# A transformer pair on one core: state products taken apart, gates issued earlier, heads scored in pairs

## The reference, cut to what matters

```
S_t = S_(t-1) diag(decay_t) + (S_(t-1) (-kk_t)) (kk_t a_t)^T + v_t k_t^T
y_t = S_t r_t
merged = sigmoid(gate_sb) * (y_sb @ w_sb_out) + sigmoid(gate_rw) * (y_rw @ w_rw_out)
h = h + merged @ w_out;   h = h + ffn(rms_norm(h));   h = rms_norm(h)
```

## Time and profile before

| what | value |
|---|---|
| three runs | 2570.83, 2576.66, 2577.05 us; median 2576.66 us |
| the profiled execution, its own time | 2576.99 us |
| its span in the profile | 2574.1 us |
| mean granted clock of TensorE | 0.981 |
| PE busy over the span | 97% |
| HBM read, written | 400.40 MB, 17.83 MB |

### The profile page before, as it was taken

How to read it: one execution, slowest core, us unless ns; L and a number is a source line. 1 busy time by engine, 2 the same in 40 slices (tenths; PEclk the granted TensorE clock), 3 DMA queues, 4 the chain that set the end, 5 groups by cost and what they waited for, 6 DMA issues and landing times.

```text
span 2574.1 us, 43775 instructions
## 1 busy us (share of the span) xinstructions
PE 2488.6 (97%) x17359; PEld 2250.1 (87%) x17359; DVE 1725.5 (67%) x3063; ACT 1248.0 (48%) x2655; POOL 534.9 (21%) x423
## 2 busy tenths in 40 slices
PE   7898999999999999999999999999999999999997
PEld 6768897999779999999888887779999999888886
DVE  4647324445668876888777555668876888777556
ACT  5441133544545454444555554555454444555554
POOL 3600142454437800000000000437700000000000
PEclk9999899999999999999999999999999999999999
DMA  5400024666325666565688666324665655777664
GB/s 172 139 9 1 18 98 155 180 185 189 119 69 152 184 184 183 182 181 182 211 244 245 196 193 190 115 82 148 186 183 183 183 181 182 213 244 240 196 192 153
DMA packets 148074, 421.07 MB, mean 164 GB/s; under 512 B 15904, under 2 KB 49056, under 8 KB 147488
## 3 DMA queue, kind: packets, MB, share of 16 engines
q1 hardware_dynamic: 144080, 405.34, 51.7%
q0 software_dynamic: 2192, 8.99, 1.0%
q10 hardware_dynamic: 1600, 3.96, 0.4%
HBM read 400.40 MB, written 17.83 MB: 162 GB/s over the span
## 4 chain that ended last, share of the span: by engine, by line
PE 86%; DVE 8%; DMA 3%; ACT 3%; issue 1%; DVEq 0%; ACTq 0%
PE pb L424 85%; DMA raw<-in_vT 2%; PE pb L433 1%; DVE arena L1475 1%; ACT arena L1054 1%; DVE arena L1478 1%; ACT hi L1042 1%; DVE lo L1485 1%; DVE arena L1625 1%; ACT L1054 0%; DMA H<-in_x 0%; DVE WL L2200 0%; DVE arena L2173 0%; DVE sm L1475 0%; DVE arena L1557 0%
## 5 line engine op out<-in xcount | busy, mean ns | idle before, releaser
L1042 ACT CAST hi<-raw 128x512 fp32r<-128x512 f32 x1402 | 816.8, 620 | 397.0 <-PE pb L424 180.8
L424 PE MATMUL pb<-HTh,hi 128*128 128x256 f32 (+1 forms) x2968 | 859.0, 289 | 0.2
L424 PE MATMUL pb<-HTl,hi 128*128 128x256 f32 (+1 forms) x2968 | 843.7, 284 | 0.0
L424 PE MATMUL pb<-HTh,lo 128*128 128x256 f32 (+1 forms) x2968 | 843.1, 284 | 0.0
L2236 POOL TENSOR_TENSOR lo<-raw,hi 128x512 fp32r<-128x512 f32 x383 | 514.0, 1364 | 646.2 <-ACT hi L1042 645.9
L1485 DVE TENSOR_TENSOR lo<-raw,hi 128x1024 fp32r<-128x1024 f32 x464 | 565.0, 1218 | 83.9 <-ACT hi L1042 83.9
L424 PEld LDWEIGHTS pb<-HTh,hi 128*128 128x128 f32 x2968 | 571.5, 193 | 2.4 <-DVE arena L1475 0.7
L424 PEld LDWEIGHTS pb<-HTl,hi 128*128 128x128 f32 x2968 | 572.1, 193 | 1.0
L424 PEld LDWEIGHTS pb<-HTh,lo 128*128 128x128 f32 x2968 | 571.2, 192 | 0.0
L424 PE MATMUL pb<-hi,WH 128*128 128x512 f32 x1112 | 434.5, 391 | 6.0 <-DVE WL L2200 6.0
L424 PE MATMUL pb<-lo,WH 128*128 128x512 f32 x1112 | 433.4, 390 | 0.0
(11 more groups left out here) (193 smaller groups left out, 2271.1 us busy)
## 6 DMA issues: line engine op xcount, KB each, us to landing
raw<-in_uT SPq DMA_DIRECT2D x256, 512.0 KB, 3.7
raw<-in_vT SPq DMA_DIRECT2D x256, 512.0 KB, 4.3
raw<-in_w_ffn_in SPq DMA_DIRECT2D x44, 512.0 KB, 3.9
raw<-in_wq SPq DMA_DIRECT2D x32, 512.0 KB, 3.7
wk<-kept SPq DMA_DIRECT2D x128, 128.0 KB, 4.2
raw<-in_w_in SPq DMA_DIRECT2D x24, 512.0 KB, 4.0
raw<-in_w_ffn_out SPq DMA_DIRECT2D x22, 512.0 KB, 4.3
raw<-in_w_gate SPq DMA_DIRECT2D x16, 512.0 KB, 3.5
```

What stands on the lines that cost most here:

```text
L424: return e.matmul(o, l, r, start=start, stop=stop)
L1042: e.copy(u.hi[k], u.half[k]).then_inc(*s.up("hi", ("hi", g)))
```

## The change

**States.** Each kind of product of the recurrence becomes a function of its own, so that products of 64 rows and products of all rows stand in separate runs. Chunk 0's states move between the levels 4, 5 and 6 of chunks 1 and 2. `rb` and `rk` get banks of their own. The copies of `y0`, `u` and chunk 0's `ST` go from DVE to ACT.

**Gates.** Three gates move ahead of the levels, one behind each chunk's pair products; three stand among the states, ten behind them, in banks that a table gives.

**Pairs.** `pair_products`, the state products of 64 rows and the scores of two heads alternate between rows 0 to 63 and rows 64 to 127. The heads are worked in the order `HEADS`, and the scores of two heads are issued together in each even step.

**Merge and query tiles.** `warm(2, 20)` goes; ACT's `mix` moves ahead of the splits of the next units. The transposes of query tiles 0 to 3 move behind `project(1, 3)` and `project(2, 0)`, into four banks, and their copies from DVE to ACT.

The core of the diff (lines of white space left out; the engines' loops over heads change from `h` to `n` and `HEADS[n]` throughout):

```diff
+HEADS = [0, 4, 1, 5, 2, 6, 3, 7, 8, 12, 9, 13, 10, 14, 11, 15]
...
+RB = {1: (0, 1), 2: (6, 7)}
+RK = {1: (2, 3), 2: (0, 1)}
+YB = {1: (2, 3), 2: (6, 7)}
+Y0B = {0: (2, 3), 1: (4, 5), 2: (4, 1)}
+GATE_BANK = (6, 7, 6, 6, 7, 0, 1, 2, 3, 0, 1, 2, 3, 0, 1, 2)
...
     def pair_products(name, i, lhs, rhs, banks):
         o, n = BLK[i]
         for par in range(2):
-            b, r = banks[par], PAR[par]
-            emptied(b)
-            for f in range(4):
+            emptied(banks[par])
+        for f in range(4):
+            for par in range(2):
+                b, r = banks[par], PAR[par]
                 x = mm(PB[b][0:n, f * n:(f + 1) * n], lhs[r, f, o:o + n], rhs[r, f, o:o + n], True, True)
-            x.then_inc(*s.up("blocks_ps", (name + "_ps", i, par)))
-            free[b] = [(name, i, par)]
-    def gate(g):
-        b = projected(units.take("gate", g), 128, 16, ("ga_ps", g))
+                if f == 3:
+                    x.then_inc(*s.up("blocks_ps", (name + "_ps", i, par)))
+                    free[b] = [(name, i, par)]
+    gates = iter(range(16))
+    def gate():
+        g = next(gates)
+        b = projected(units.take("gate", g), 128, 16, ("ga_ps", g), GATE_BANK[g])
         free[b] = [("ga", g)]
     for i in range(3):
         pair_products("mt", i, m.BT, m.AT, (0, 1))
         pair_products("x", i, m.AT, m.BT, (2, 3))
         pair_products("lt", i, m.KT, m.AT, (4, 5))
+        gate()
...
+    def y0_rows(i):
+        n = BLK[i][1]
+        w.wait_ge(*s.to("n", i, 1))
+        for par in range(2):
+            b = Y0B[i][par]
+            emptied(b)
+            for f, h in heads_of(par):
+                x = mm(PB[b][0:n, f * 64:f * 64 + 64], m.mat(i, LTk)[:, h, :], m.NN[0:n, 2, i, HC[h]], i == 0 or f == 0, i == 0)
+            if i == 0:
+                x.then_inc(*s.up("state_ps", ("y0_ps", i, par)))
+                free[b] = [("y0", i, par)]
...
+    def y0_state(i):
+        s0, n = BLK[i]
+        w.wait_ge(*s.to("st", i - 1))
+        for f in range(4):
+            for par in range(2):
+                b = Y0B[i][par]
+                x = mm(PB[b][0:n, f * 64:f * 64 + 64], m.AT[PAR[par], f, s0:s0 + n], m.ST[PAR[par], f, :], False, f == 3)
+                if f == 3:
+                    x.then_inc(*s.up("state_ps", ("y0_ps", i, par)))
+                    free[b] = [("y0", i, par)]
...
+    def solved(i, b):
+        n = BLK[i][1]
+        emptied(b)
+        w.wait_ge(*(s.to("n", i, 7) if i else s.to("n", 0, 4)))
+        w.wait_ge(*s.to("y0", i, 1))
+        for h in range(8):
+            x = mm(PB[b][0:n, HC[h]], m.mat(i, XTk)[:, h, :], m.Y0[0:n, HC[h]], True, True)
+        x.then_inc(*s.up("state_ps", ("u_ps", i)))
+        free[b] = [("u", i)]
...
+    def state_rows(i, b):
+        n = BLK[i][1]
+        emptied(b)
+        for h in range(8):
+            dst = PB[b][PAR[h % 2], h // 2 * 64:h // 2 * 64 + 64]
+            mm(dst, m.NN[0:n, 1, i, HC[h]], m.NN[0:n, 2, i, HC[h]], h < 2, False)
+    def state_solved(i, b):
+        n = BLK[i][1]
+        w.wait_ge(*s.to("u", i))
+        for h in range(8):
+            dst = PB[b][PAR[h % 2], h // 2 * 64:h // 2 * 64 + 64]
+            x = mm(dst, m.NN[0:n, 0, i, HC[h]], m.UU[0:n, HC[h]], False, h > 5)
+        x.then_inc(*s.up("state_ps", ("st_ps", i)))
+        free[b] = [("st", i)]
...
+    def yt_state(i):
+        s0, n = BLK[i]
+        for par in range(2):
+            emptied(YB[i][par])
+        w.wait_ge(*s.to("st", i - 1))
+        for f in range(4):
+            for par in range(2):
+                mm(PB[YB[i][par]][PAR[par], f * 128:(f + 1) * 128], m.ST[PAR[par], f, :], m.RT[PAR[par], f, s0:s0 + n], f == 0, False)
+    def yt_rows(i):
+        n = BLK[i][1]
+        for par in range(2):
+            w.wait_ge(*s.to("rk", i, par))
+            for f, h in heads_of(par):
+                mm(PB[YB[i][par]][PAR[par], f * 128:(f + 1) * 128], m.NN[0:n, 2, i, HC[h]], m.mat(i, RKk)[:, h, :], False, False)
+    def yt_solved(i):
+        n = BLK[i][1]
+        w.wait_ge(*s.to("u", i))
+        for par in range(2):
+            w.wait_ge(*s.to("rb", i, par))
+            for f, h in heads_of(par):
+                x = mm(PB[YB[i][par]][PAR[par], f * 128:(f + 1) * 128], m.UU[0:n, HC[h]], m.mat(i, RBk)[:, h, :], False, f == 3)
+            x.then_inc(*s.up("state_ps", ("yt_ps", i, par)))
...
     for lv in range(1, 7):
-        for i in (1, 2):
-            level(i, lv)
+        level(1, lv)
+        if lv == 4:
+            y0_rows(0)
+        elif lv == 5:
+            solved(0, 3)
+        elif lv == 6:
+            state_rows(0, 3)
+            state_solved(0, 3)
+        level(2, lv)
         if lv < 4:
             level(0, lv)
-    for i in (1, 2):
-        w.wait_ge(*s.to("n", i, 7))
-        pair_products("rb", i, m.BT, m.RT, (0, 1))
-        pair_products("rk", i, m.KT, m.RT, (2, 3))
-    gates = 0
-    for i in range(3):
-        o, n = BLK[i]
-        for par in range(2):
-            r = PAR[par]
-            emptied(par)
-            w.wait_ge(*(s.to("rk", i, 1) if i else s.to("n", 0, 4)))
-            if i:
-                w.wait_ge(*s.to("st", i - 1))
-            for f in range(4):
-                h = 2 * f + par
-                dst = PB[par][0:n, f * 64:f * 64 + 64]
-                if i:
-                    mm(dst, m.AT[r, f, o:o + n], m.ST[r, f, :], True, False)
-                x = mm(dst, m.mat(i, LTk)[:, h, :], m.NN[0:n, 2, i, HC[h]], i == 0, True)
-            x.then_inc(*s.up("state_ps", ("y0_ps", i, par)))
-            free[par] = [("y0", i, par)]
-        if i:
-            gate(gates)
-            gates += 1
-        emptied(2)
-        w.wait_ge(*s.to("y0", i, 1))
-        for h in range(8):
-            x = mm(PB[2][0:n, HC[h]], m.mat(i, XTk)[:, h, :], m.Y0[0:n, HC[h]], True, True)
-        x.then_inc(*s.up("state_ps", ("u_ps", i)))
-        free[2] = [("u", i)]
-        if i:
-            gate(gates)
-            gates += 1
-            for par in range(2):
-                b, r = 4 + par + 2 * (i - 1), PAR[par]
-                emptied(b)
-                for f in range(4):
-                    h = 2 * f + par
-                    dst = PB[b][r, f * 128:(f + 1) * 128]
-                    mm(dst, m.ST[r, f, :], m.RT[r, f, o:o + n], True, False)
-                    mm(dst, m.NN[0:n, 2, i, HC[h]], m.mat(i, RKk)[:, h, :], False, False)
-                    w.wait_ge(*s.to("u", i))
-                    x = mm(dst, m.UU[0:n, HC[h]], m.mat(i, RBk)[:, h, :], False, True)
-                x.then_inc(*s.up("state_ps", ("yt_ps", i, par)))
-                free[b] = [("yt", i, par)]
-        if i < 2:
-            emptied(3)
-            for h in range(8):
-                f, r = h // 2, PAR[h % 2]
-                dst = PB[3][r, f * 64:f * 64 + 64]
-                mm(dst, m.NN[0:n, 1, i, HC[h]], m.NN[0:n, 2, i, HC[h]], True, False)
-                w.wait_ge(*s.to("u", i))
-                x = mm(dst, m.NN[0:n, 0, i, HC[h]], m.UU[0:n, HC[h]], False, True)
-            x.then_inc(*s.up("state_ps", ("st_ps", i)))
-            free[3] = [("st", i)]
-    for _ in range(3):
-        gate(gates)
-        gates += 1
+    y0_rows(1)
+    y0_state(1)
+    pair_products("rb", 1, m.BT, m.RT, RB[1])
+    pair_products("rk", 1, m.KT, m.RT, RK[1])
+    w.wait_ge(*s.to("n", 2, 7))
+    pair_products("rb", 2, m.BT, m.RT, RB[2])
+    solved(1, 4)
+    pair_products("rk", 2, m.KT, m.RT, RK[2])
+    gate()
+    yt_state(1)
+    state_rows(1, 5)
+    state_solved(1, 5)
+    gate()
+    yt_rows(1)
+    yt_solved(1)
+    y0_rows(2)
+    y0_state(2)
+    yt_state(2)
+    yt_rows(2)
+    solved(2, 5)
+    gate()
+    yt_solved(2)
+    for _ in range(2):
...
-    warm(2, 20)
...
         for f in range(4):
-            turn_tile(f, 2 + f % 2, ("qa", l))
-        project(1, 3, 6)
-        for g in range(2):
-            project(2, g, 4)
+            turn_tile(f, f, ("qa", l))
+        project(2, 1, 4)
         turn_tile(4, 2, ("ka", l))
...
+        def at_scores(n):
+            pair = HEADS[n:n + 2]
+            for b, h in enumerate(pair):
+                f = 5 * (h // 8)
+                emptied(b)
+                w.wait_ge(*s.to("qt", l, f + h % 4))
+                w.wait_ge(*s.to("qt", l, f + 4))
             for t in range(2):
-                x = mm(PB[b][:, t * 256:(t + 1) * 256], m.QT[r, f + j, t * 128:(t + 1) * 128], m.QT[r, f + 4, :], True, True)
-            x.then_inc(*s.up("score_ps", ("score_ps", l, h)))
-            free[b] = [("nmx", l, h)] if g else [("px", l, h)]
-        def at_turn(h):
-            i, b = h % 3, 2 + h % 2
+                for b, h in enumerate(pair):
+                    r, f = PAR[h % 8 // 4], 5 * (h // 8)
+                    x = mm(PB[b][:, t * 256:(t + 1) * 256], m.QT[r, f + h % 4, t * 128:(t + 1) * 128], m.QT[r, f + 4, :], True, True)
+                    if t:
+                        x.then_inc(*s.up("score_ps", ("score_ps", l, h)))
...
         take("gate", g)
-        b = bank()
```

(112 more changed lines are left out.)

163 lines of the change are left out of this document (69 added, 94 removed).

## The result

The changed kernel takes 2586.5 us, median of 6 runs (2581.0 to 2589.1), against 2575.4 for the kernel before, 6 runs beside it. The ratio is 1.0044, 95% interval 1.003 to 1.0057: slower by 0.44%, some 11 us. The forecast was 2519, range 2503 to 2542. The profiled execution has a span of 2585.1 us.

A forecast was written before the change was run, and what follows sets the result against it. The prediction took PE, busy 97%, to bound most of the kernel, with DVE bounding the masks. States and gates 38.8, merge 8.0 and attention 11.2 sum to 58.0, from 2577.0 to 2519 us, range 2503 to 2542.

The forecast's parts named there:

- States and gates: Recurrence and gates ahead of the first FFN: 33.5 us saved on states plus 5.7 on gates less 0.4, 38.8.
- The 70.05 of the earlier trace: From the levels' end to chunk 2's last `yt`: 70.05 us was to become 32.1, plus 4.4 in the levels.
- the low end: `yt_rows` and `yt_solved` behind the levels: 3.5 us in place of 7.0 if both parities' column halves run at once.
- 2.6 in place of 0.4: Three early gates among DVE's masks: 0.4 us was the predicted cost of what PE's free time does not cover.
- PE has 4.7 free: Mask stretch, 189.80 to 204.00: DVE bounds it, PE has 4.7 us free towards the three early gates' 8.5.
- The merge: Product with `w_out` behind the states: without the filler it can start when PE has done `rwo(3)`, 8.0 us gained.
- The attention: Each layer's attention: 1.8 front, 1.4 and 0.4 from pairs, 2.0 at the end; 5.6 us a layer, 11.2 in all.
- the 5.0: Attention heads, steps 4 to 8: PE was to need 5.0 us for a pair where two heads took 6.1.
- Rival (b): Attention gives nothing, second heads wait on DVE and PE meets banks 0 and 1 unread: 2530 us, chance 0.14.
- (e): Rival: clock at 0.50 through the levels and some states, +56 us, 2575 and beyond that slower, 2580; chance 0.03.
- The 1.86 between the query tiles: Ahead of the attention's scores: PE's wait of 1.86 us goes, part of the 1.8 gained a layer at the front.

The follow-up runs named there:

- filler_odd: The changed kernel with the filler of the attention's head loop at odd steps only, seven groups a layer left out: 2516.0 us, ratio 0.9768 to before.
- filler_ahead: The changed kernel with all its head-loop fillers, those at even steps issued ahead of the pair's scores: 2523.3 us, ratio 0.9804 to before.
- plant: The kernel before with one edit, the head loop's filler put into the bank that the step's scores were just written to: 2657.5 us, ratio 1.0311.

## Why the prediction was wrong

**States and gates, right.** Predicted 38.8, measured 38.0. By stretch, for the levels and from their end to the last `yt` of chunk 2:

```profile
221.73:283.68 61.95, 60.78 (x648) 59.08 (x648) 39.09 (x58) 14.94 (x32) 0.00 (x0) 1.00 0.01 2
283.68:312.71 29.03, 29.03 (x345) 27.43 (x344) 7.16 (x10) 8.06 (x18) 7.58 (x6) 1.00 0.12 37
```

The 70.05 of the earlier trace rows became 29.03 behind the levels, predicted 32.1, and 5.4 more in the levels (61.95 against 56.51), predicted 4.4: 34.5 against 36.5. No clock below 1.00, no wait of PE in levels 4 to 6. Of the 3.1 less behind the levels, 1.7 are in `yt_rows` and `yt_solved`, priced at 7.0 and measured at 5.3 (2.49, 1.51 and 1.31):

```profile
298.59:301.08 2.49, 2.49 (x33) 2.32 (x32) 0.00 (x0) 0.76 (x2) 0.00 (x0) 1.00 0.43 171
303.01:304.05 1.04, 1.04 (x17) 0.97 (x16) 0.00 (x0) 0.00 (x0) 0.00 (x0) 1.00 0.00 0
305.07:306.58 1.51, 1.51 (x18) 1.34 (x16) 0.00 (x0) 0.00 (x0) 0.00 (x0) 1.00 0.00 0
```

`yt_rows` and `yt_solved` of chunk 1 take 2.5 for 32 records, 1.5 for the 16 of chunk 2: less than the 0.11 a record that I took, more than the half of it that I kept for the low end. The 16 of `y0_state`, in pairs, take 1.0 (0.9 predicted). The 2.0 gained on my sum and the 2.2 lost in the masks (2.6 in place of 0.4) nearly cancel, so that 38.0 lies so near 38.8 is partly luck. The failed step in the small: "PE has 4.7 free", which counted PE's queue and neither POOL's nor the 1.2 us that DVE waits for a gate.

**The merge, right in size.** Where the product with `w_out` ends (395.58 against 442.16), 8.6 more are gained than at its first transfer (8.0 predicted). Behind the FFN 6.8 remain, since the next turn waits 1.5 us for DVE in place of 0.6, and the rest is lost behind it. As the prediction read the rows: no gap ahead of the product, and a clock of 1.00 from 370.2 to 378.0.

**The attention, wrong.** The step that failed is "From step 4 to 8 PE had no pause, and a step is 0.50 turn, 0.54 filler, 2.0 for values and scores. In pairs PE needs 5.0 for 6.1." It prices the filler as 0.54 of work and gives it no wait. I had seen the filler's bank cost 4.88 in the merge and did not ask which bank it meets in the loop. The runs put in its place: 26.3 us of waits in layer 0's attention, and records at a clock of 0.84. With the wait taken away, the total comes near: from the FFN to the first `uT` transfer `filler_odd` gains 6.8 and 7.4 in the two layers, 5.6 predicted, and its 2516.0 lies beside the 2519 of the sum. But that is in part luck, since `filler_odd` has seven filler groups a layer less than the change whose price I worked out. `filler_ahead` has them all, gains 1.2 and 3.4 there, and takes 2523.3. And the 5.0 were what PE needs for a pair, which is not what bounds it: from step 4 on the pairs stand 6.0 to 7.3 apart in `filler_odd`, by the starts of ACT's exponentials, as two heads did before (6.1 to 7.4). Rival (b) named the place (banks 0 and 1 unread in each even step) and priced it at nothing gained; none of the rivals ended with a loss in the attention. The only one on the slower side, (e), put it in the levels, where the clock stayed at 1.00.

The 1.86 between the query tiles did go, in the changed kernel too. There a stretch at half clock (0.51 from 606.80 to 610.20) took the gain back before the first scores; in `filler_odd` 1.9 and 2.3 stand.

## What to carry to other kernels

When a change fills a buffer earlier or fills two at once, look at every other user of that buffer, those whose result is thrown away above all: a filler inherits every wait of the bank that it writes. A work item that moves takes its preparation on the other engines with it, so count the queues that it passes (here POOL's subtractions over DVE's masks), not only the engine that was free. And when an engine's work is made cheaper, ask whether it was the one that bound the stretch. A filler belongs where its bank has been read already and nobody waits behind it: seven groups in the right place beat fourteen, and beat none.

## What the hardware showed that I had not expected

- Small waits can cost more by the clock than by themselves: in `plant` waits of 10.4 us, none above 1.4, came with 38 us of slower records at 0.66, in the changed kernel waits of 26 us with about 15 at 0.84.
- DVE and POOL: beside POOL's subtraction a DVE product of two SBUF operands of 128x1024 took 2.2 for 1.23, one of 16x128 took 1.25 for 0.28, and a 128x272 operation with one SBUF tensor and scalars took 1.28 for 0.36. The delay is about 1 us in each of these, whatever the size of DVE's own operation.
- Less work for PE need not be less time: the scores in pairs took 7.5 us off PE's busy time a layer, and the stretch lost 0.8.
- Products into 64 columns of the array, four of one half and then four of the other, overlap in part: 32 records of 128 rows took 2.49, 0.08 each, where one after another 0.11 each was read in the earlier trace rows.
